# Two block products of a seven-product unit accumulated in the PSUM banks of two others

## What is computed

```python
def half_ffn(x, shift, scale, gate, w_in, w_out, g, b):
    h = modulate(x, shift, scale)
    a, u = jnp.split(h @ w_in, 2, axis=-1)        # w_in: 1024 x 5632, a and u: 2816 wide
    y = (jax.nn.silu(a) * u) @ w_out              # w_out: 2816 x 1024
    return layernorm(ALPHA * x + 0.5 * gate * y, g, b)
```

## Time and profile before

| | |
|---|---|
| median of 3 runs | 2866.28 us (2865.33 to 2867.95) |
| profiled execution | 2870.56 us, of it the span from first to last instruction 2868.9 us |
| mean granted TensorE clock | 0.994 of full speed |
| PE matmul busy | 2802.6 us, 98% of the span, 17130 instructions |
| VectorE busy | 1993.4 us, 69%, 3238 instructions |
| ScalarE busy | 1026.9 us, 36% |
| DMA | 267.20 MB, mean 93 GB/s |
| chain that ended last | PE 91%, DVE 4%, DMA 2% |

### The profile page before, as it was taken

The page is one execution under the profiler, slowest core; times in us unless marked ns, Lnnn a source line. Parts: engine busy times, 40 slices in busy tenths (PEclk is TensorE's granted clock), DMA queues, the critical chain, the costliest instruction groups (busy, mean ns, idle before and its releaser), DMA issues.

```text
span 2868.9 us, 45992 instructions
## 1 busy us (share of the span) xinstructions
PE 2802.6 (98%) x17130; PEld 2445.9 (85%) x17130; DVE 1993.4 (69%) x3238; ACT 1026.9 (36%) x1618; POOL 323.9 (11%) x421
## 2 busy tenths in 40 slices
PE   7999999999999999999999999999999999999998
PEld 3888999988867888989998899999978998878886
DVE  4776777766766676776677877777767886655544
ACT  3322232345621422322225233233256665422222
POOL 1101000111100000010010000000205553000001
PEclk9999999999999999999999999999999999999999
DMA  9434332212232244344421222222310101233331
GB/s 344 150 118 163 130 95 66 73 60 63 59 114 65 70 146 147 124 155 138 154 66 45 66 66 66 66 66 77 87 42 25 27 19 45 86 106 95 95 102 45
DMA packets 303282, 267.20 MB, mean 93 GB/s; under 512 B 30775, under 2 KB 260027, under 8 KB 303035
## 3 DMA queue, kind: packets, MB, share of 16 engines
q1 hardware_dynamic: 280538, 186.40, 21.8%
q0 software_dynamic: 21760, 76.03, 7.4%
q10 hardware_dynamic: 864, 3.15, 0.3%
HBM read 260.30 MB, written 5.24 MB: 93 GB/s over the span
## 4 chain that ended last, share of the span: by engine, by line
PE 91%; DVE 4%; DMA 2%; ACT 1%; issue 1%; POOL 0%; SPq 0%; DVEq 0%; POOLq 0%; ACTq 0%
PE PSALL L2993 15%; PE PSALL L2994 15%; PE PSALL L2995 15%; PE PSALL L3311 8%; PE PSALL L3312 8%; PE PSALL L3313 8%; PE PSALL L3069 2%; PE PSALL L2914 2%; PE PSALL L3070 2%; PE PSALL L3071 2%; PE PSALL L3739 2%; PE PSALL L3724 1%; PE PSALL L3022 1%; PE PSALL L3604 1%; PE PSALL L3582 1%
## 5 line engine op out<-in xcount | busy, mean ns | idle before, releaser
L2101 DVE SCALAR_TENSOR_TENSOR X<-PSALL,GATE,X 128x512 f32<-128x512 f32 x480 | 280.2, 612 | 107.4 <-PE PSALL L2995 106.8
L3311 PE MATMUL PSALL<-HHI,WSH 128*128 128x384 f32 x816 | 275.2, 337 | 4.1 <-DVE U L2126 2.8
L3312 PE MATMUL PSALL<-HLO,WSH 128*128 128x384 f32 x816 | 274.0, 336 | 0.0
L3313 PE MATMUL PSALL<-HHI,WSL 128*128 128x384 f32 x816 | 273.7, 335 | 0.0
L2993 PE MATMUL PSALL<-GHIA,WHIW 128*128 128x512 f32 (+1 forms) x618 | 217.4, 352 | 11.0 <-DVE X L2101 6.8
L2994 PE MATMUL PSALL<-GLOA,WHIW 128*128 128x512 f32 (+1 forms) x618 | 213.6, 346 | 0.0
L2995 PE MATMUL PSALL<-GHIA,WLOW 128*128 128x512 f32 (+1 forms) x618 | 213.1, 345 | 0.0
L2993 PE MATMUL PSALL<-GHIB,WHIW 128*128 128x512 f32 (+1 forms) x618 | 212.8, 344 | 0.0
L2995 PE MATMUL PSALL<-GHIB,WLOW 128*128 128x512 f32 (+1 forms) x618 | 212.6, 344 | 0.0
L2994 PE MATMUL PSALL<-GLOB,WHIW 128*128 128x512 f32 (+1 forms) x618 | 212.6, 344 | 0.0
L1230 ACT ACTIVATE WSH<-RAW 128x512 fp32r<-128x512 f32 x204 | 129.0, 632 | 230.4 <-DVE RAW L2178 158.7
(11 more groups left out here) (431 smaller groups left out, 7070.4 us busy)
## 6 DMA issues: line engine op xcount, KB each, us to landing
RAW<-in_ffn_w_in_dram SPq DMA_DIRECT2D x176, 512.0 KB, 4.4
ADA<-in_ada_w_dram POOLq DMA_DIRECT2D x128, 512.0 KB, 5.7
RAW<-in_ffn_w_out_dram SPq DMA_DIRECT2D x88, 512.0 KB, 3.7
RAW<-in_ev_w_in_dram SPq DMA_DIRECT2D x20, 512.0 KB, 3.9
ADAF<-in_ada_w_dram POOLq DMA_DIRECT2D x16, 512.0 KB, 10.5
WRAW<-in_mla_w_q_up_dram SPq DMA_DIRECT2D x16, 288.0 KB, 3.0
RAW<-in_ev_w_out_dram SPq DMA_DIRECT2D x8, 512.0 KB, 4.1
RAW<-in_mla_w_in_dram SPq DMA_DIRECT2D x8, 512.0 KB, 4.8
```

The costliest lines, as they stand in the source:

```text
L2101: dve.scalar_tensor_tensor(X[:, m, lo:lo + n], down_bank(m, s, 2), GATE[:, j, m, s:s + 1], X[:, m, lo:lo + n], ALU.mult, ALU.add).then_inc ...
L3311: te.matmul(out, w_hi, hi[block](k), start=(k == 0), stop=False)
L3312: te.matmul(out, w_hi, low[block](k), start=False, stop=False)
L3313: x = te.matmul(out, w_lo, hi[block](k), start=False, stop=(k == 3))
```

## The change

The seven products come in another order, and two of them are added to the result of an earlier one in PSUM: 21 onto 11 in bank b (fourth), and 22 onto T1 in bank b + 1 (last); `seventh` gets `add`, with which the first matmul doesn't reset the bank. T3 goes to b + 2 (third) and T4 to b (sixth). `gate_first` and `fourth_sum` are gone; `silu_first` reads PSUM bank b and writes the first half of GM. A unit has five sums instead of seven, and all counts follow. raw_hi waits for product 4 instead of 3; `between()` stands behind product 4. TensorE waits for silu_first ahead of T4, and for up_second (g_add 3) ahead of 22. Ahead of the third row product behind a B unit it waits for third_sum, where it waited for up_first.

```diff
@@ ScalarE, wide @@
             def silu_first(slot, i):
 
-                act.wait_ge(g_add, 7 * seven(name, slot, i) + 2)
-                act.activation(GM[slot][:, 0:HALF], GM[slot][:, 0:HALF], ACT.Silu).then_inc(silu[slot], 1)
+                act.wait_ge(glo[slot], (p.g if slot == "A" else p.gB) + i)
+                act.wait_ge(g_pe, 5 * seven(name, slot, i) + 4)
+                act.activation(GM[slot][:, 0:HALF], PS[0 if slot == "A" else 3][:, 0:HALF], ACT.Silu).then_inc(silu[slot], 1)
...
-                raw_hi(n, q, i, (g_pe, 5 * v + 3))
+                raw_hi(n, q, i, (g_pe, 5 * v + 4))
@@ VectorE, wide @@
-            def gate_first(slot, i):
-
-                dve.wait_ge(g_pe, 5 * seven(name, slot, i) + 3)
-                dve.tensor_tensor(GM[slot][:, 0:HALF], PS[2 if slot == "A" else 5][:, 0:HALF], P1[:, :],
-                                  ALU.add).then_inc(g_add, 1)
...
-                dve.wait_ge(g_pe, 5 * v + 4)
-                dve.wait_ge(g_add, 7 * v + 1)
-                dve.tensor_tensor(U3[:, :], PS[0 if slot == "A" else 3][:, 0:HALF], GM[slot][:, HALF:TOK],
+                dve.wait_ge(g_pe, 5 * v + 3)
+                dve.wait_ge(g_add, 5 * v + 1)
+                dve.tensor_tensor(U3[:, :], PS[2 if slot == "A" else 5][:, 0:HALF], GM[slot][:, HALF:TOK],
                                   ALU.add).then_inc(g_add, 1)
...
-            def fourth_sum(slot, i):
+            def up_second(slot, i):
 
                 v = seven(name, slot, i)
                 dve.wait_ge(g_pe, 5 * v + 5)
-                dve.wait_ge(g_add, 7 * v + 3)
-                dve.tensor_tensor(GM[slot][:, HALF:TOK], PS[1 if slot == "A" else 4][:, 0:HALF], GM[slot][:, HALF:TOK],
-                                  ALU.add).then_inc(g_add, 1)
-
-            def up_second(slot, i):
-
-                v = seven(name, slot, i)
+                dve.wait_ge(g_add, 5 * v + 2)
                 dve.tensor_tensor(P1[:, :], PS[1 if slot == "A" else 4][:, 0:HALF], U3[:, :], ALU.add).then_inc(g_add, 1)
...
-                gate_first(slot, i)
                 if late:
                     late()
                 low_first()
                 third_sum(slot, i)
                 difference()
-                fourth_sum(slot, i)
                 up_second(slot, i)
@@ TensorE, wide @@
-                seventh(1, "21", b + 2).then_inc(g_pe, 1)
+                seventh(2, "T3", b + 2).then_inc(g_pe, 1)
+                te.wait_ge(g_p1, v + 1)
+                seventh(1, "21", b, add=True).then_inc(g_pe, 1)
                 if between is not None:
                     between()
-                te.wait_ge(g_p1, v + 1)
-                seventh(2, "T3", b).then_inc(g_pe, 1)
-                te.wait_ge(g_add, 7 * v + 1)
+                te.wait_ge(g_add, 5 * v + 1)
                 seventh(3, "T1", b + 1).then_inc(g_pe, 1)
-                te.wait_ge(g_add, 7 * v + 2)
+                te.wait_ge(silu[slot], p.gs + 2 * i + 1)
                 te.wait_ge(t_lo, 10 * blk + 8)
-                seventh(6, "T4", b + 2).then_inc(pe[slot], 1)
-                te.wait_ge(g_add, 7 * v + 3)
+                seventh(6, "T4", b).then_inc(pe[slot], 1)
+                te.wait_ge(g_add, 5 * v + 3)
                 te.wait_ge(lo_done, q + 2 + 6 * i)
-                seventh(5, "22", b).then_inc(pe[slot], 1)
+                seventh(5, "22", b + 1, add=True).then_inc(pe[slot], 1)
...
-                     taken=lambda: te.wait_ge(g_add, 7 * seven(name, "B", i) + 6))
+                     taken=lambda: te.wait_ge(g_add, 5 * seven(name, "B", i) + 2))
```

More of the change, by code:

```diff
@@ L1206, in silu_first @@
             def silu_first(slot, i):
-                act.wait_ge(g_add, 7 * seven(name, slot, i) + 2)
-                act.activation(GM[slot][:, 0:HALF], GM[slot][:, 0:HALF], ACT.Silu).then_inc(silu[slot], 1)
+                act.wait_ge(glo[slot], (p.g if slot == "A" else p.gB) + i)
+                act.wait_ge(g_pe, 5 * seven(name, slot, i) + 4)
+                act.activation(GM[slot][:, 0:HALF], PS[0 if slot == "A" else 3][:, 0:HALF], ACT.Silu).then_inc(silu[slot], 1)
             def silu_second(slot, i):
-                act.wait_ge(g_add, 7 * seven(name, slot, i) + 7)
+                act.wait_ge(g_add, 5 * seven(name, slot, i) + 5)
                 act.activation(GM[slot][:, HALF:TOK], GM[slot][:, HALF:TOK], ACT.Silu).then_inc(silu[slot], 1)
@@ L2139, in up_second @@
                 v = seven(name, slot, i)
+                dve.wait_ge(g_pe, 5 * v + 5)
+                dve.wait_ge(g_add, 5 * v + 2)
                 dve.tensor_tensor(P1[:, :], PS[1 if slot == "A" else 4][:, 0:HALF], U3[:, :], ALU.add).then_inc(g_add, 1)
@@ L2145, in up_first @@
                 dve.wait_ge(pe[slot], (p.A if slot == "A" else p.B) + 2 * i + 1)
-                dve.wait_ge(g_add, 7 * v + 5)
-                dve.tensor_tensor(U3[:, :], PS[2 if slot == "A" else 5][:, 0:HALF], U3[:, :], ALU.add).then_inc(g_add, 1)
+                dve.wait_ge(g_add, 5 * v + 3)
+                dve.tensor_tensor(U3[:, :], PS[0 if slot == "A" else 3][:, 0:HALF], U3[:, :], ALU.add).then_inc(g_add, 1)
             def gated_first(slot, i):
-                dve.wait_ge(g_add, 7 * seven(name, slot, i) + 6)
+                dve.wait_ge(g_add, 5 * seven(name, slot, i) + 4)
                 dve.wait_ge(silu[slot], p.gs + 2 * i + 1)
@@ L2156, in gate_second @@
                 dve.wait_ge(pe[slot], (p.A if slot == "A" else p.B) + 2 * i + 2)
-                dve.tensor_tensor(GM[slot][:, HALF:TOK], PS[0 if slot == "A" else 3][:, 0:HALF], GM[slot][:, HALF:TOK],
+                dve.tensor_tensor(GM[slot][:, HALF:TOK], PS[1 if slot == "A" else 4][:, 0:HALF], GM[slot][:, HALF:TOK],
                                   ALU.add).then_inc(g_add, 1)
@@ L2398, in wide @@
             split_lo("W", 0, p.q + 6 * last, 0)
-            gate_first("A", last)
             rebuild_mix(0)
@@ L2402, in wide @@
             split_lo("W", 1, wide_q(name, "W1", last), last)
-            fourth_sum("A", last)
             up_second("A", last)
@@ L3304, in up_classic, with seventh @@
                     x.then_inc(pe[slot], 1)
-            def seventh(place, block, bank):
+            def seventh(place, block, bank, add=False):
                 out = PS[bank][:, 0:HALF]
@@ L3310, in seventh @@
                     w_hi, w_lo = (t[:, place, P * k:P * k + P] for t in (WSH, WSL))
-                    te.matmul(out, w_hi, hi[block](k), start=(k == 0), stop=False)
-                    te.matmul(out, w_hi, low[block](k), start=False, stop=False)
-                    x = te.matmul(out, w_lo, hi[block](k), start=False, stop=(k == 3))
+                    te.matmul(out, w_hi, hi[block](k), start=(k == 0 and not add), stop=False, skip_group_check=add)
+                    te.matmul(out, w_hi, low[block](k), start=False, stop=False, skip_group_check=add)
+                    x = te.matmul(out, w_lo, hi[block](k), start=False, stop=(k == 3), skip_group_check=add)
                 return x
```

1 line of the change is left out of this document (removed).

## The result

The changed kernel takes 2891.38 us (median of 4 runs, 2890.04 to 2893.88), the kernel before 2866.10 (4 runs, 2865.33 to 2867.95): 1.0088 times as long, 95% interval 1.0076 to 1.0100, or 25 us more. The profiled execution took 2890.04 us, its span 2888.4, with a mean granted clock of 0.992.

What follows compares the result with a forecast made beforehand. TensorE's queue alone was taken as the bound, VectorE beside it. 15.6 us in ordinary units plus 1.9 in first units made 17.5: 2888 for the profiled execution, 2884 as median, range 2873 to 2898.

Steps and rivals of the forecast that it cites:

- The steady term: Product 7's wait for up_second in 34 ordinary units, 0.46 us each (bounds 0.34 to 0.70), 15.6 us in all.
- The chain: silu_first, raw_hi, low_first, third_sum, difference, up_second in turn: up_second ends at 248.84, where TensorE wants product 7 at 248.60.
- Which units pay: 24 B units and 10 A units without adaLN work from i = 3 on pay; last A units of stages don't.
- Later groups have 0.5 us or more in hand: Row products behind the fifth: they were to have enough cover not to wait for accumulate.
- The two delays are one and not two: Product 7's delay already moves the fifth row product to about 255.34, when accumulate lets it count; 0.24 us more as bound.
- The restart charge: After product 7's wait, its second matmul comes 0.28 us behind the first instead of 0.17, counted as 0.10 us.
- The rule that the prediction weighed against it: Weight loads pulled ahead across product 7's wait would save 0.10 us: 14.1 us in sum instead of 17.5.
- The first units: First unit of three stages, product 7 behind difference's weight DMA: +1.9 us in sum, bounds -2 and +10.
- Worth nothing in the 48 units: Removing 102 VectorE sums, 48 us of its queue, gains nothing in the 48 units where TensorE doesn't wait.
- Late, but hidden: Rival, 7%: up_second ends 0.55 us sooner than found, product 7 loses nothing; 2866 plus or minus 3.
- VectorE's backlog at the first units: Rival, 4%: fewer sums clear TensorE's waits of 2.8 and 6.8 us there; faster, 2856.
- AdaLN's loads: Forecast: DMAs issued 2.10 us later cost nothing. Rival, 5%: too late, 1 us in each of 13 units, 2897.

Runs made afterwards that it cites:

- e6: Changed kernel with the adaLN products put back between product 3 and 4: 2892.33 us, 1.0091 times the kernel before.
- e1: Changed kernel with up_second ahead of difference in VectorE's queue: 2891.54 us, 1.0086 times the kernel before.
- e4: Changed kernel with only 21 added onto 11; 22 gets its own bank and fourth_sum stays: 2898.71 us, 1.0108 times the kernel before.
- e8: The kernel of e3 with the adaLN products back between product 3 and 4: 2862.49 us, 0.9983 times the kernel before.
- e5: Kernel before with only 22 added onto T1 (fourth_sum gone), its product order and gate_first kept: 2872.81 us, 1.0021 times the kernel before.
- e3: Changed kernel with third_sum ahead of low_first, difference behind up_second, and on ScalarE raw_hi ahead of silu_first: 2867.36 us, 1.0003 times the kernel before.
- e7: The kernel of e5 with difference moved behind up_second: 2862.63 us, 0.9985 times the kernel before.
- e10: Kernel before, all seven sums kept, with difference moved behind up_second: 2871.73 us, 1.0015 times the kernel before.
- e11: The same kernel as e7, run once more beside e10: 2863.46 us, 0.9988 times the kernel before.

## Why the prediction was right, and where it wasn't

**The steady term.** 34 units at 0.46 us were predicted, 15.6 in all; 34 waits came, at 0.41 and 13.7 to 13.9 in all. The chain held step by step (first table). Product 7's delay and the restart are 0.33 + 0.12 = 0.45, as computed; the 0.05 of difference are mostly products 4 and 5, which follow the ones ahead of them 0.02 sooner each, where the prediction took them as unchanged.

**Which units pay.** A units with adaLN work behind product 4 were predicted to pay nothing. They don't, and e6, which takes that cover away, has 48 waits instead of 37. The last A unit of a stage was to pay nothing either, since low_first and difference aren't in its queue. Product 7 doesn't wait there, but its "Later groups have 0.5 us or more in hand" fails in this unit: the seventh row product waits, and each of the three pays 0.55 us, 1.7 in all, for a gated_second of 1.82 us beside GpSimd's L894. GpSimd's share in that unit was not looked at.

**"The two delays are one and not two."** Confirmed from both sides: in the changed kernel the fifth row product doesn't wait in ordinary units, and where product 7's wait is taken away (e1, e4) it appears there, at 0.7 to 0.8 us with what these edits add to the queue.

**The restart charge.** By the row the stalled product's second matmul came 0.28 us behind the first; it did, 251.88 to 252.16. The rule that the prediction weighed against it, that weight loads are pulled ahead of matmuls in flight (the Trainium skill, TensorE: Matmul & The Clock Gate, Part 2: What happens when you issue a matmul), did not save this 0.10 here: the row decided rightly.

**The first units: the mis-sized term.** Predicted +1.9 (bounds -2 and +10), measured +8.0. The mechanism was there: product 7 waits for up_second behind the DMA-bound difference, and most of its delay goes into the wait of the fifth row product. In ffn0 the fifth row product was to come 1.3 us later in the unit; it came 6.2 later (32.3 us behind product 1's start instead of 26.1). Two things were left out. First, the DMA of difference takes 2.3 us longer, as adaLN's loads now lie beside it for longer; e6 and e8 show that it ends when they are moved back. Second, behind the long wait TensorE runs at half clock, so that from product 7's start to the fifth row product 11.0 us pass instead of the 8.3 to 8.45 of units without that wait: +2.6. 1.3 + 2.3 + 2.6 = 6.2. Of this the two spacings behind it give back 1.7, which were slow before, too: 4.5, against 4.56 measured. In ffn2, without adaLN work, -0.7 was predicted and +0.74 measured; product 7 took 3.75 us instead of 2.2, +1.6 for the clock. That a wait costs its length, and that adaLN's later loads cost nothing, are the steps that failed. (The lower bound of -2 is also too near by its own working: three times 0.94 is 2.8. It decided nothing.)

**"Worth nothing in the 48 units."** Of the sums removed, that is right where the order leaves cover: e5, in the order of the kernel before, has one sum a unit fewer and the same ordinary units (+0.1 in all), and e3, in an order of its own, has 102 sums fewer and the time of before. It isn't right in general: e7 against e10 shows 8 us, won by one sum fewer where the order has no cover left.

**The rivals.** "Late, but hidden" needed up_second 0.55 us sooner; it came 0.04 sooner. The rival on the other side, VectorE's backlog at the first units, was there in size (e8 takes 6.7 us from them, of the 10 named), but it needs the order of e8; in the changed kernel up_second is held by the chain and by the DMA, as the prediction said it must not be. AdaLN's loads are waited for 0.4 us in all. The whole lies within the range, 7 us above the predicted 2884: the first units are 6.1 more than computed, the last A units 1.7 more and the ordinary ones 1.9 less, and the rest, under 2 us, is not located. Part of the closeness is luck: two misses of one sign, 6.1 and 1.7, are offset by one of the other.

## What to carry to other kernels

An accumulation in PSUM saves a sum on an engine that may have time to spare, and delays whatever read the first product alone. Before fusing, follow the reader's engine: whatever is queued behind an instruction that now waits is late too, so put what is ready ahead of it, and keep instructions that read each other's result apart. Where a load or a wait moves, ask also whom it delays, and count a long wait of TensorE at more than its length (here those of 4.5 and 6.45 us). An engine that gets work sooner can get in another's way: look at what starts beside it.

## What the runs showed of the hardware

- After a wait of 6.45 us the granted clock was 0.50 for 4.0 us and 0.55 for 2.0 more; after one of 4.5 us (e5) product 7 took 4.0 us as well. In ffn1 of the changed kernel product 7 took 3.64 us. A last wait of 1 us (e1, product 7 of ffn0) was followed by full speed, while a spacing of some 4.25 us at the same place in ffn2 was followed by a slow product 7 in e7 (3.75) and by a normal one in e1 (2.21) and in e11 (2.20), which is the same kernel as e7. So the length of the last wait alone doesn't say whether the clock falls; what else does is open.
- VectorE starts an independent instruction 0.47 us behind a 128x384 sum of 0.55, and one that waits for and reads its result 0.66 behind it; behind a 128x512 difference of 0.68 it is 0.60 (changed kernel) and 0.72 (e1, e10).
- A 128x384 product of two SBUF tiles on VectorE took 0.55 us by itself, and 1.82 where a GpSimd copy of 1.47 us had started 0.06 us ahead of it. Where VectorE's started first, the copy took longer instead, 1.66 us before and 1.80 in e5.
- A load of 512 KB took 3.75 us without adaLN's loads (ffn2, before), 4.94 with 3.5 us of them beside it (ffn0, before) and 7.24 with 5.8 us (ffn0, changed kernel).
